# Conditioning chunks of a two-block transformer kernel: twelve ahead of the experts, eight behind them, four ahead of the second gate and up projection

## What is computed

```
def second_block(x, c, w_ada, b_ada, norm1_g, norm2_g, w_in, ..., w_out, w_gate_up, w_down):
    mod = silu(c) @ w_ada + b_ada
    sh1, sc1, g1, sh2, sc2, g2 = split(mod, 6)
    hn = rms(x, norm1_g) * (1 + sc1) + sh1
    y = mixer(hn, w_in, ...)
    x = x + g1 * (y @ w_out)
    hn = rms(x, norm2_g) * (1 + sc2) + sh2
    gate, up = split(hn @ w_gate_up, 2)
    return x + g2 * ((silu(gate) * up) @ w_down)
```

## Time and profile before

| | us |
|---|---|
| median of three runs | 1482.58 |
| the profiled execution | 1481.83 |
| its span, first to last instruction | 1479.9 |
| TensorE busy in the span | 1418.5 |
| experts, first gate and up to last scatter | about 145 to 1060 |

### The profile page before, as it was taken

The page is one execution under the profiler, slowest core; times in us unless marked ns, Lnnn a source line. Parts: engine busy times, 40 slices in busy tenths (PEclk is TensorE's granted clock), DMA queues, the critical chain, the costliest instruction groups (busy, mean ns, idle before and its releaser), DMA issues.

```text
span 1479.9 us, 17841 instructions
## 1 busy us (share of the span) xinstructions
PE 1418.5 (96%) x7196; PEld 756.2 (51%) x7196; DVE 364.0 (25%) x937; ACT 222.3 (15%) x417; POOL 21.7 (1%) x14
## 2 busy tenths in 40 slices
PE   7998999999999999999999999999899997999999
PEld 5654444444444443344334433433388855888843
DVE  4546421121121121121112111211325562003400
ACT  1431011011011011011101110111213442000000
POOL 3200000000000000000000000000000000000000
PEclk9999999999999999999999999999999998999999
DMA  9979999999999999999999999999994222444300
GB/s 336 349 295 426 418 428 428 427 429 428 428 428 428 428 430 428 429 428 429 428 429 428 429 428 429 428 429 429 404 328 141 92 89 98 149 143 149 135 0 28
DMA packets 82719, 497.03 MB, mean 336 GB/s; under 512 B 6253, under 2 KB 47930, under 8 KB 54682
## 3 DMA queue, kind: packets, MB, share of 16 engines
q1 hardware_dynamic: 82076, 495.46, 82.2%
q10 hardware_dynamic: 606, 1.06, 0.2%
HBM read 495.44 MB, written 1.05 MB: 336 GB/s over the span
## 4 chain that ended last, share of the span: by engine, by line
PE 71%; DMA 23%; DVE 3%; issue 1%; ACT 1%; SPq 0%; DVEq 0%; ACTq 0%
PE PS L920 17%; DMA ring<-in_w_gate_up_dram 15%; PE PS L946 11%; PE PS L1281 10%; DMA qk<-in_w_gate_up_dram 8%; PE PS L1049 6%; PE PS L905 6%; PE PS L1288 5%; PE PS L954 3%; PE PS L639 2%; PE PS L1165 2%; PE PS L742 1%; PE PS L622 1%; PE PS L932 1%; PE PS L914 1%
## 5 line engine op out<-in xcount | busy, mean ns | idle before, releaser
L920 PE MATMUL PS<-ring,store 128*64 128x512 f32 x1360 | 301.0, 594 | 14.8 <-DMA ring<-in_w_gate_up_dram 14.3
L920 PEld LDWEIGHTS PS<-ring,store 128*64 128x64 f32 x1360 | 94.4, 137 | 208.7 <-issue 170.5
L2015 DVE TENSOR_SCALAR store<-PS 128x512 f32<-128x512 f32 x32 | 22.1, 691 | 627.7 <-PE PS L920 627.7
L1281 PE MATMUL PS<-xc,ring 128*128 128x256 f32 x704 | 155.3, 384 | 2.1 <-issue 2.1
L946 PE MATMUL PS<-ring,store 128*64 128x512 f32 x704 | 154.8, 592 | 0.0
L1281 PEld LDWEIGHTS PS<-xc,ring 128*128 128x128 f32 x704 | 135.8, 193 | 21.9 <-DVE xc L1718 2.5
L905 PE MATMUL PS<-store,rows 128*128 128x64 f32 x1056 | 125.2, 272 | 1.2 <-DVE store L1993 1.2
L905 PEld LDWEIGHTS PS<-store,rows 128*128 128x128 f32 x1056 | 123.4, 192 | 2.1 <-DVE store L1993 2.1
L946 PEld LDWEIGHTS PS<-ring,store 128*64 128x64 f32 x704 | 49.3, 137 | 90.7 <-issue 89.1
L1049 PE MATMUL PS<-ring,xc 128*128 128x240 f32 (+1 forms) x448 | 93.6, 366 | 0.5 <-issue 0.5
L1445 ACT ACTIVATE store<-store 128x512 f32<-128x512 f32 x32 | 20.1, 629 | 452.8 <-DVE store L2015 452.8
(11 more groups left out here) (304 smaller groups left out, 1143.7 us busy)
## 6 DMA issues: line engine op xcount, KB each, us to landing
ring<-in_w_gate_up_dram SPq DMA_DIRECT2D x85, 2048.0 KB, 35.0
ring<-in_w_down_dram SPq DMA_DIRECT2D x44, 2048.0 KB, 38.0
qk<-in_w_gate_up_dram SPq DMA_DIRECT2D x21, 2048.0 KB, 37.5
ring<-in_w_ada_dram SPq DMA_DIRECT2D x24, 1024.0 KB, 15.7
store<-in_w_gate_up_dram SPq DMA_DIRECT2D x11, 2048.0 KB, 35.7
ring<-in_w_gate_up_dram SPq DMA_DIRECT2D x22, 1024.0 KB, 5.0
xc<-in_w_down_dram SPq DMA_DIRECT2D x10, 2048.0 KB, 36.8
store<-in_w_down_dram SPq DMA_DIRECT2D x10, 2048.0 KB, 38.2
```

The source lines that it names most:

```text
L920: mm = pe.matmul(bank(b)[CAP * h:CAP * (h + 1), :], xg[:, k, :], w[:, b * FE + h * 512:b * FE + (h + 1) * 512], start=False, stop=(k == KD ...
L1281: mm = pe.matmul(bank(4 + 2 * (j % 2) + up)[:, f * T:(f + 1) * T], chunk(n)[:, k, f * P:(f + 1) * P], cols[:, k, :], start=(k == 0), stop= ...
L2015: v.tensor_scalar(g_min, bank(0), LIMIT, None, ALU.min).then_inc(clipped, 1)
```

## The change

Twelve conditioning chunks instead of eighteen now stand ahead of the experts, eight instead of six behind them, and four stand between the second output projection and `turn_rows(9)`. The third column group is cut otherwise: chunks 16 to 23 hold two row tiles by 1024 columns (`sc2` in 16 to 19, `g2` in 20 to 23). Their matmuls write the two row tiles into separate rows of the bank, so that two rows of `mod` have to be added: VectorE adds the transposed columns of `sc2`, and `spread_halves` adds those of `g2` with four matmuls in place of two. `mod` gets a fourth plane, its biases come in six transfers instead of four, and `wpool` moves into `spare`. Behind the experts the chunks use banks 0 and 1, and the rows are transposed into banks 4 to 7; the wait there is for `x_squared` 5 instead of 3. The last four use bank 5. `turn_mod(1)` moves from the router to behind the first input chunk.

```diff
-ADA_CHUNKS = [(g, k) for g in range(3) for k in range(KD)]
+ADA_CHUNKS = [(g, k) for g in range(2) for k in range(KD)] + [(g, k) for g in (2, 3) for k in range(0, KD, 2)]
-ADA_SEGMENTS = (0, 6, 8, 12, 16, 18, 24)
+ADA_SEGMENTS = (0, 6, 8, 10, 12, 16, 20, 24)
+ADA_BANK = (7, 7, 7, 7, 0, 1, 5)
-N_OUT1B = N_OUT1 + 2 + 6
-N_MOE = N_OUT1B + 2 + 6
+N_OUT1B = N_OUT1 + 2 + 4
+N_MOE = N_OUT1B + 2 + 2
-N_IN2 = N_AFTER + 6
+N_IN2 = N_AFTER + 8
-N_GU2 = N_OUT2 + 4
+N_GU2 = N_OUT2 + 4 + 4
...
             values_1(3)
-            ada(10)
-            ada(11)
...
-            ada(12)
-            ada(13)
+            ada(10)
+            ada(11)
             pe.wait_ge(sig["x_added"], 1)
             turn_mod(0, 6)
-            ada(14)
-            ada(15)
...
-            ada(16)
...
-            ada(17)
...
-            turn_mod(1, 3)
-            pe.wait_ge(sig["ada_kept"], 5)
+            pe.wait_ge(sig["ada_kept"], 4)
             add_x(7)
...
+            for i in range(12, 18):
+                ada(i)
             pe.wait_ge(sig["z_ready"], 4)
-            pe.wait_ge(sig["x_squared"], 3)
-            ada(18)
-            ada(19)
-            ada(20)
-            turn_rows(6, between=(21,))
-            ada(22)
-            ada(23)
+            pe.wait_ge(sig["x_squared"], 5)
+            turn_rows(6, between=(18, 19), base=4)
             need_cols()
...
+            def spread_halves(g, banks):
+                for h, b in enumerate(banks):
+                    for j in (h, h + 2):
+                        mm = pe.matmul(bank(b), ident[:, 32 * j:32 * j + 1].to_broadcast([P, P]), mod[:, g, :],
+                                       start=(j == h), stop=(j > h))
+                mm.then_inc(sig["bcast_done"], 1)
...
                 if c == 0:
+                    turn_mod(1, 7)
                     turn_mod(2, 6)
...
             out2(1, 7, (1,))
+            for i in range(20, 24):
+                ada(i)
             turn_rows(9)
...
                 if j == 1:
-                    spread(2, 2, (0, 1))
+                    spread_halves(3, (0, 1))
```

More of the change, by code:

```diff
@@ L500, in _ @@
                     for j in range(4):
-                        load_small(mod[32 * j:32 * j + 32, :, :],
-                              ins["b_ada_2"][0].rearrange("(g j n) -> j g n", g=3, j=4)[j].partition_broadcast(32),
+                        load_small(mod[32 * j:32 * j + 32, 0:2, :],
+                              ins["b_ada_2"][0][0:4 * D].rearrange("(g j n) -> j g n", g=2, j=4)[j].partition_broadcast(32),
+                              "bada_in")
+                    for j in range(2):
+                        load_small(mod[32 * j:32 * j + 32, 2:4, :],
+                              ins["b_ada_2"][0][4 * D:6 * D].rearrange("(g j n) -> j g n", g=2, j=2)[j].partition_broadcast(32),
                               "bada_in")
@@ L584, in _, with turn_rows @@
             turned = [0]
-            def turn_rows(wait_rows, by_tile=True, between=()):
+            def turn_rows(wait_rows, by_tile=True, between=(), base=0):
                 for t in range(NT):
@@ L591, in turn_rows @@
                     for k in range(KD):
-                        mm = pe.transpose(bank(k // 2)[:, (k % 2) * T + t * P:][:, 0:P],
+                        mm = pe.transpose(bank(base + k // 2)[:, (k % 2) * T + t * P:][:, 0:P],
                                           rows[:, t, k * P:(k + 1) * P], ident)
@@ L616, in ada @@
                     pe.wait_ge(sig["c_ready"], 1)
-                elif i == ADA_SEGMENTS[segment]:
+                elif i == ADA_SEGMENTS[segment] and ADA_BANK[segment] == 7:
                     pe.wait_ge(sig["ada_kept"], segment)
+                elif i == ADA_SEGMENTS[-2]:
+                    pe.wait_ge(sig["gate_used"], 2)
                 n = ADA_AT[i]
@@ L621, in ada @@
                 for j in range(4):
-                    mm = pe.matmul(bank(7)[32 * j:32 * j + 32, :], c_rep[:, k, :], slot(n)[:, j * 512:(j + 1) * 512],
+                    mm = pe.matmul(bank(ADA_BANK[segment])[32 * j:32 * j + 32, :],
+                                   c_rep[:, k + j // 2 if i >= 16 else k, :], slot(n)[:, j * 512:(j + 1) * 512],
                                    start=(i in ADA_SEGMENTS), stop=(i + 1 in ADA_SEGMENTS))
@@ L1817, in keep_ada @@
                 g = ADA_CHUNKS[lo][0]
-                dve.wait_ge(sig["bada_in"], 64)
+                dve.wait_ge(sig["bada_in"], 96)
                 dve.wait_ge(chunk_used, ADA_AT[hi - 1] + 1)
-                do.tell(v.tensor_tensor(mod[:, g, :], bank(7), mod[:, g, :], ALU.add), "ada_kept")
+                do.tell(v.tensor_tensor(mod[:, g, :], bank(ADA_BANK[segment]), mod[:, g, :], ALU.add), "ada_kept")
             def row_max(i, head):
@@ L1969, in _ @@
             do.tell(v.tensor_copy(small[:, 4:6], small[:, 0:2]), "shifted")
-            keep_ada(4)
             dve.wait_ge(sig["exp_ready"], 2)
@@ L2095, in _ @@
                         "rows_ready")
-            keep_cols(lambda k: modg[:, k:k + 1], lambda k: modc[:, k:k + 1])
+            keep_cols(lambda k: modg[:, k:k + 1], lambda k: modc[:, k:k + 1], base=4)
+            keep_ada(4)
             keep_ada(5)
@@ L2260, in _ @@
             keep_cols(lambda k: modg[:, 8 + k:9 + k], lambda k: modc[:, 24 + k:25 + k])
+            keep_ada(6)
             for j in range(PAIRS):
```

29 lines of the change are left out of this document (18 added, 11 removed).

## The result

| | us |
| --- | --- |
| before, median of 13 runs | 1483.73 (1480.65 to 1486.04) |
| after, median of 13 runs | 1488.01 (1483.74 to 1491.52) |
| ratio | 1.0026, 95% interval 1.0014 to 1.0039 |
| profiled execution, before and after | 1481.83, 1485.27 |
| its span, before and after | 1479.9, 1483.3 |

By the ratio the change makes the kernel slower by 3.9 us (2.1 to 5.8; the medians differ by 4.3), a little over what can be told from no change. The profiled pair differs by 3.4 us. The forecast was 1484.7 us with a range up to 1487.7, against a median of before of 1482.58; over 13 runs that median is 1483.73. On the forecast's scale the ratio gives 1482.58 x 1.0026 = 1486.4, near the slow end of the range; the median of 1488.01 itself lies 0.3 us above it.

The account below looks back on a forecast made before the run. The expert weights stream was taken as the bound. Stream and start +0.55, eighth chunk +1.2, `turn_mod` +0.6, spread +1.7, clock at the end -1.15, together +2.9 on 1481.83: 1484.7 us, range 1479.3 to 1487.7.

Parts of the forecast that it names:

- the cost of the fall: From the router into the first expert: half clock costs 4.2 us, bounds 2.5 and 6, 0 if the clock holds.
- the shorter queue: At the first expert slot given back: 1.75 us less weight transfer still queued, credited to the experts' end.
- TensorE reaches the output projection earlier: Ahead of the experts: six conditioning chunks fewer bring TensorE there sooner, -1.9 us together.
- The clock falls in the stretch of transposes: At the router: 6.9 us of only transposes and waits would drop TensorE's granted clock to 0.50.
- Rival (a): At the router the clock holds, so 4.2 us go: 1480.5 us (1478.5 to 1482); chance 0.25.
- The experts' end: End of the expert weight stream: first slot 2.3 us later, less 1.75 us queued, gives +0.55 us.
- Rival (b): In the experts, the weight stream keeps its whole gain of 14.7 us: 1469.5 us; chance 0.07.
- The eighth chunk: Behind the experts: TensorE waits for this conditioning chunk's landing between the row tiles, +1.2 us (bounds 0 and 2).
- `turn_mod`: In the dense projection behind the experts: its four transposes, moved from a wait at the router, cost about +0.6 us.
- The spread: At the end, in dense work: four matmuls in `spread_halves` where two stood, +1.7 us.
- The clock at the end: Around the last transposes and final projection: a shorter stretch without matmuls saves 1.15 us (bounds -3.55 and 0).
- Rival (c): Ahead of the second block's projection the clock falls a second time: 1487.1 us (1486 to 1489); chance 0.16.

Follow-up runs that it names:

- experiment 11: Changed kernel plus matmuls that nobody reads inside the three waits at the router; median 1484.49 us (11 runs), ratio 1.0004.
- experiment 5: Kernel before plus matmuls that nobody reads ahead of the first projection, at the router and around the last transposes; median 1487.61 us (7 runs), ratio 1.0038.
- Experiment 12: Changed kernel with chunk 19 behind the transposes, one spread matmul a bank, unread matmuls in the router's and end's waits; median 1477.08 us (6 runs), ratio 0.9949.
- after again: The changed kernel profiled and timed a second time, with nothing altered; median 1491.17 us (5 runs), ratio 1.0051.

## Why the prediction was right, and where it was not

**The forecast's sign and size held in the profiled pair, in part by luck: the cost of the fall was too small, and two savings, 1.75 us for the shorter queue and 1.15 at the end, were too large.** By steps:

- *TensorE reaches the output projection earlier.* -1.9 forecast; the output projection stands 102.84 - 44.88 = 57.96 us from the pair, before 105.13 - 45.32 = 59.81: -1.85. Right.
- *The clock falls in the stretch of transposes.* It did, in all seven profiles of the changed kernel with no fillers among the transposes (the one with the delayed slot has some ahead of the gather), for 13 to 21 us. Right. What the prediction did not know is that before pays some of this too: of its three profiles with the router as it was, one had 7.0 us at half clock there and its slot at 106.56. Rival (a), 1480.5 us (1478.5 to 1482) if the clock holds, is what experiment 11 made: ratio 1.0004, about 1483, above the rival's bounds, since it too counted on the 1.75 and the 1.15 (its first 64 records at the end took 16.92 us, no less than before's).
- *What the fall costs: mis-sized.* Forecast 4.2 (bounds 2.5 to 6). In the profiled pair the slot is 3.29 us later from the pair although TensorE came 1.85 earlier: 5.1. The split was wrong more than the sum. For the transposes, the router's product and the logits I had 1.8 us: from output projection to the router's product there are 26.45 us in both kernels, and from there to the gather 8.90 against 8.26, so 0.6. From the gather's start to the first expert there are 147.75 - 138.19 = 9.56 us against 144.93 - 139.84 = 5.09: 4.5, where I took 2.4, because I let the clock come back within the gather; it came back at its end or in the first expert. Against experiment 11, which has no fall, the slots of the changed kernels come 5.1 to 6.6 us later.
- *The experts' end: the step that failed.* The prediction credited the 1.75 us less of queued work at the first slot to the end of the experts. I took 2.3 us for the slot and gave 1.75 back for the shorter queue, +0.55. Measured +2.20, or +2.64 from the pair. The landing was as predicted (7.8 us; 7.45 forecast), but the end of the experts follows the slot's issue, not its landing: it comes 891.2 to 892.4 us behind the issue in fourteen profiles, whose first landings lie between 7.6 and 9.3 us, and the two don't go together (correlation 0.03). On average it is 891.53 us in the four profiles of before and 891.56 in the six of the changed kernel with nothing added at the router: nothing of the 1.75 is left. Of the 1.4 us that the first landing gained in the profiled pair, the transfer issued 86.5 us behind the slot has 0.7 left (before, then after), and the end 0.65:

```profile
ring<-in_w_down_dram SPq DMA_DIRECT2D x1, 2048.0 KB, 17.5
ring<-in_w_down_dram SPq DMA_DIRECT2D x1, 2048.0 KB, 16.8
```

What the end does follow beside the issue is this transfer: over the fourteen profiles it lands after 16.7 to 17.6 us, and the 891.2 to 892.4 go with it (correlation 0.98). So the difference of 1.2 us is there 86.5 us behind the slot and stays; what makes it in these first experts no row shows.
- *Rival (b), the whole stream kept,* fell as the landing of 9.2 us said: six MiB fewer gave the end of the experts no gain.
- *The eighth chunk,* +1.2: +1.24, and -1.23 when it was moved. `turn_mod`, +0.6: the second chunk of that projection starts 3.88 us later where the first was 3.44 later, +0.44. *The spread,* +1.7: 3.44 - 1.71 = +1.73. All right.
- *The clock at the end,* -1.15: in the profiled pair the final projection starts 0.66 earlier against the work before it and its first 64 records take 1.49 less, -2.15. That was luck: over the seven changed kernels with this part unfilled those 64 take 15.5 to 17.1 us, 16.4 on average, before 16.96 and 16.07. With them the term is -0.66 - 0.1 = -0.8. Mis-sized by 0.35.
- *Rival (c), a second fall ahead of the second block's projection,* did not come in the profiled run, but in four of the nine others of the changed kernel there were 3.4 us at half clock between 1060 and 1090, and in three of before's four there were 3.4, 6.8 and 10.2 (the last around the idle 5.13 us of experiment 5). It is no property of the change.

With the measured sizes the sum is: slot +2.7 (mean of six changed kernels, 107.1 with the fall near 68 us taken off, less the mean of three of before, 104.4), 1.24 + 0.44 + 1.73 - 0.8 = +5.3 us. The two measurements have +3.9 (2.1 to 5.8) and +7.5 (5.6 to 9.5, 5 runs). So the forecast of +2.9 was some 2 us short, and nearly all of that is the experts' end: +2.7 measured for +0.55. The profiled pair hid it, by the luck at its end: 2.20 + 1.24 + 0.44 + 1.73 - 2.15 = 3.46, its 3.4 us.

**Where the expected gain went.** Chunks taken away ahead of the experts removed transfers that had time, and matmuls that helped to keep TensorE's clock up: there before had 0 to 7.0 us at half clock in its four profiles, the changed kernel 13 to 21 in seven. Experiment 12 kept the first and replaced the second.

## What to carry to other kernels

The weight stream here had to wait for the first free slot, and ended the same time behind it to within 1.2 us: where a stream stands still like this, count how early the slot comes, not how many bytes are gone ahead of it. Work that hides in a wait may still be holding the clock; before taking it away look at the granted clock, and if it falls, put matmuls into the waits, not beside them. One profile shows one draw of the clock: take a second of both kernels, and the mean granted clock of every run, before pricing a fall.

## What was not expected of the hardware

- The fall of the clock differs from one execution to the next: for the unchanged before, time at half clock was 15 to 39 us over 24 runs and the time 1480.2 to 1493.0 us, going together. In six runs of the kernel without falls it was 0 to 9 us.
- A half-clock stretch lasted between 3.4 and 13.7 us. In dense matmuls the clock took up to 6.2 us to come back (the gate and up projection of after again, from 1252.1 to 1258.3), and around the gather, where waits stand between, the stretch was up to 13.7 us.
- The matmul behind the skipped branch waited 5.13 us in one kernel, whose only difference from before at that place is that more instructions stand ahead of it. The Trainium skill, "Runtime: NRT & Kernel Launch", Instruction fetch mechanics, says that a taken branch to a target outside the pages at hand waits for a fetch. That fits, but no run here moved the branch alone; it stays open.
